# Two-layer decoder step on one core: VectorE instead of GpSimd forms the weight-block sums of the down phases, and the ends of the MLP phases are reordered

## What is computed

```python
x = x + mix                                   # output projection of the mixer
h = rmsnorm(x, p['norm_mlp'][layer])
x = x + jnp.square(jax.nn.relu(h @ p['mlp_up'][layer])) @ p['mlp_down'][layer]   # 1024 -> 4096 -> 1024
# layer 0: h = rmsnorm(x, p['norm_mix'][1]) and the projections of layer 1's mixer follow
# layer 1: y = rmsnorm(x, p['norm_final']) follows, and is the output
```

## Time and profile before

| | us |
|---|---|
| median of 3 runs | 3350.61 (3347.99 to 3360.74) |
| the profiled execution, time | 3352.3 |
| its span | 3350.2 |
| PE busy | 3192.0 (95%) |
| DVE busy | 2122.2 (63%) |
| ACT busy | 1165.8 (35%) |
| POOL busy | 1279.1 (38%) |
| mean granted clock of PE | 0.977 |

### The profile page before, as it was taken

One profiled execution on the slowest core, in us unless ns is written; L12 is line 12 of the kernel. 1 busy time (PEld: TensorE's weight loads), 2 busy tenths in 40 slices (PEclk: granted clock), 3 DMA queues, 4 the chain that ended last, 5 costly groups with the idle time before them and its releaser, 6 DMA issues. The chain is left out here.

```text
span 3350.2 us, 74980 instructions
## 1 busy us (share of the span) xinstructions
PE 3192.0 (95%) x31716; PEld 3017.6 (90%) x31716; DVE 2122.2 (63%) x2892; ACT 1165.8 (35%) x2373; POOL 1279.1 (38%) x760
## 2 busy tenths in 40 slices
PE   8999889999999988999999989999998999999997
PEld 7999768888887888999999989999998899999997
DVE  5112874664665748666777784566546966667776
ACT  3344122332332334444333342221222444443333
POOL 3322120110113025444677733222211544457783
PEclk9999899999999999999999989999999999999998
DMA  5113630100011102444544411111112144454442
GB/s 170 59 58 109 190 118 9 33 30 16 30 36 48 67 30 74 142 143 143 201 147 146 131 46 57 66 63 59 59 60 112 58 137 145 143 199 144 144 146 82
DMA packets 151199, 322.70 MB, mean 96 GB/s; under 512 B 16904, under 2 KB 50356, under 8 KB 150744
## 3 DMA queue, kind: packets, MB, share of 16 engines
q1 hardware_dynamic: 106480, 242.53, 22.3%
q10 hardware_dynamic: 44392, 75.42, 6.6%
HBM read 227.12 MB, written 93.12 MB: 96 GB/s over the span
## 5 line engine op out<-in xcount | busy, mean ns | idle before, releaser
L247 PE MATMUL psum<-act_hi,w_hi 128*128 128x352 f32 x2088 | 704.7, 337 | 21.2 <-DVE act_lo L4169 5.7
L232 POOL TENSOR_TENSOR w_hi<-w_raw,derived 128x1024 fp32r<-128x1024 f32 x87 | 169.4, 1947 | 1415.6 <-PE psum L247 1339.3
L247 PE MATMUL psum<-act_hi,w_lo 128*128 128x352 f32 x2088 | 677.7, 325 | 0.0
L247 PE MATMUL psum<-act_lo,w_hi 128*128 128x352 f32 x2088 | 676.6, 324 | 0.0
L247 PEld LDWEIGHTS psum<-act_hi,w_hi 128*128 128x128 f32 x2088 | 397.1, 190 | 49.8 <-issue 15.2
L247 PEld LDWEIGHTS psum<-act_lo,w_hi 128*128 128x128 f32 x2088 | 398.7, 191 | 2.5 <-issue 0.2
L247 PEld LDWEIGHTS psum<-act_hi,w_lo 128*128 128x128 f32 x2088 | 397.9, 191 | 0.0
L1072 PE MATMUL psum<-ff_near,ff_w_hi 128*128 128x264 f32 x2048 | 382.7, 287 | 8.9 <-ACT ff_a L1202 5.9
L1072 PEld LDWEIGHTS psum<-ff_near,ff_w_hi 128*128 128x128 f32 x2048 | 320.0, 190 | 15.5 <-issue 15.1
L1072 PE MATMUL psum<-ff_far,ff_w_hi 128*128 128x264 f32 x1536 | 285.9, 287 | 12.3 <-DVE ff_r L1407 6.2
L1072 PE MATMUL psum<-ff_near,ff_w_lo 128*128 128x264 f32 x1024 | 292.7, 286 | 0.0
(11 more groups left out here) (556 smaller groups left out, 7496.5 us busy)
## 6 DMA issues: line engine op xcount, KB each, us to landing
ff_du_raw<-u SPq DMA_DIRECT2D x224, 264.0 KB, 2.8
w_raw<-weights SPq DMA_DIRECT2D x87, 512.0 KB, 3.3
u<-ff_stage SPq DMA_DIRECT2D x128, 264.0 KB, 2.2
ff_raw<-mlp SPq DMA_DIRECT2D x64, 512.0 KB, 3.9
u<-ff_side SPq DMA_DIRECT2D x96, 264.0 KB, 3.7
s_cache<-cache_a ACTq DMA_DIRECT2D x32, 512.0 KB, 6.8
ff_dt<-mlp SPq DMA_DIRECT2D x64, 256.0 KB, 4.4
ff_dt<-mlp SPq DMA_DIRECT2D x32, 512.0 KB, 7.1
```

The lines of the kernel that those rows point to most:

```text
L232: pool.tensor_tensor(hi, raw, self.zeros, ALU.add).then_inc(s.sem, s.step())
L247: last = pe.matmul(out, w[:, k, :], h[:, k, cols], start=(start and k == ks[0] and m == 0), stop=(stop and k == ks[-1] and m == 2))
```

## The change

It has five parts. The tables and orders that only say which row comes when are shown by two lines.

1. **Down phases**: DVE forms all sums of weight blocks (S1 to S4, all groups). They stand behind the adds of a step: S1 and S3 of the first group behind step 0, S1 of the next group behind a group's last step, S3 behind its first, S2 behind the step ahead of product 1, S4 behind the step ahead of product 6. POOL is left with the low parts of weights.
2. **Start of the down phase**: the four `u_lower` of step 1 stand ahead of step 0's adds, and `mixed_last` of the last pair behind step 0's third unit.
3. **Steps 26 and 27**: their high and low parts get buffers of their own ("last") and are written ahead, those of step 27 into DVE's step 25.
4. **First pair of the up phase**: DVE makes the low parts for P5, P3 and P4; the eighth row of squares is no longer added by DVE but by PE (two float32 matmuls for each of the three sums); the quadrants come in the order 22, 12, 11, 21; ACT keeps ff_a of pair 1 ahead of squaring quadrant 21, and ff_b of pair 15 ahead of squaring quadrant 11; POOL waits for the last operand of P4 before it starts on pair 1.
5. **Around the MLPs**: the first four weight tiles of layer 1's mixer are loaded into four buffers during step 25, ACT makes their high parts, POOL the low parts by one subtraction each. The squares of the norm behind either MLP are added in another order, and the final norm takes the middle norm's order.

```diff
     def column_sum(self, engine, steps, g, q):
...
-    def corner_sum(self, pool, g, q):
+    def corner_sum(self, dve, g, q):
...
-        pool.tensor_tensor(a11, self.S1[q][:, :], a11, ALU.subtract).then_inc(steps.sem, steps.step(f"split.{n}.S2_{g}.{q}"))
+        dve.tensor_tensor(a11, self.S1[q][:, :], a11, ALU.subtract).then_inc(steps.sem, steps.step(f"dve.{n}.S2_{g}.{q}"))
...
     def pool(self, pool):
...
         for p in (1, 2, 6, 7):
             self.weight_low(pool, 0, p)
-        for p in (5, 3, 4):
-            self.weight_low(pool, 0, p)
+        pool.wait_ge(*at(f"dve.{n}.lo_T4_1"))
         for w in range(1, self.PAIRS):
...
         for step in range(self.STEPS):
-            g, m = divmod(step, 7)
-            for q in four:
+            for q in range(self.WIDTH):
                 self.w_lower(pool, step, q)
-            if step == 1 or m == 6 and g + 1 < self.GROUPS:
-                for q in four:
-                    self.side_sum(pool, s, 0 if step == 1 else g + 1, q)
-            if g and m == 0:
-                for q in four:
-                    self.column_sum(pool, s, g, q)
-            if self.product_of(step) == 1:
-                for q in four:
-                    self.corner_sum(pool, g, q)
-            if self.product_of(step) == 6:
-                for q in four:
-                    self.row_sum(pool, g, q)
...
     def pe_sum(self, pe):
...
-            pe.matmul(K.psum[:, 6 + c % 2, 0:TC], K.ones[:, :], self.rstd[:, c * TC:(c + 1) * TC], start=True, stop=True)\
-                .then_inc(s.sem, s.step(f"pe.{n}.sum{c}"))
+            cols, out = slice(c * TC, (c + 1) * TC), K.psum[:, 6 + c % 2, 0:TC]
+            pe.matmul(out, K.ones[:, :], self.rstd[:, cols], start=True, stop=False)
+            pe.matmul(out, K.ones[:, :], self.sq_last[:, cols], start=False, stop=True).then_inc(s.sem, s.step(f"pe.{n}.sum{c}"))
...
     def act(self, act):
...
-        for p in (3, 4):
-            self.weight_high(act, 1, p)
+        keep_both(1, 0)
         self.square_out(act, 0, "21")
+        self.weight_high(act, 1, 4)
...
-        self.square_out(act, w, "11")
         self.w_high(act, 0, 1)
         keep_both(w, 1)
+        self.square_out(act, w, "11")
...
+        end, last = self.STEPS - 2, self.STEPS - 1
+        for q in range(self.WIDTH):
+            self.w_high(act, end, q)
         for q in range(2):
-            self.w_high(act, self.STEPS - 1, q)
+            self.w_high(act, last, q)
         for q in range(self.WIDTH):
-            self.u_high(act, self.STEPS - 1, q)
-            if q >= 2:
-                self.w_high(act, self.STEPS - 1, q)
+            self.u_high(act, end, q)
+        for q in range(2, 4):
+            self.w_high(act, last, q)
+        for q in range(self.WIDTH):
+            self.u_high(act, last, q)
+        if self.following is not None:
+            self.following.act_weights(act)
...
     def dve_step(self, dve, k, c):
...
-        add(7)
         self.weight_sum(dve, 0, 4)
...
+        for p in (5, 3):
+            self.weight_low(dve, 0, p)
...
     def dve(self, dve):
...
-        self.mixed_last(dve, w)
+        for q in range(self.WIDTH):
+            self.u_lower(dve, 1, q)
         for step in range(self.STEPS - 2):
             for j, d in enumerate(self.UNITS):
                 self.down_add(dve, step, d)
-                if j < 2:
-                    for q in (2 * j, 2 * j + 1):
+                if step == 0 and j == 2:
+                    self.mixed_last(dve, w)
+                for q in (2 * j % 4, 2 * j % 4 + 1):
+                    if 0 < step and j < 2:
                         self.u_lower(dve, step + 1, q)
-            if step == 0:
-                for q in range(self.WIDTH):
-                    self.column_sum(dve, s, 0, q)
+                    elif step == self.STEPS - 3:
+                        self.u_lower(dve, step + 2, q)
+            g, m = divmod(step, 7)
+            p = self.product_of(step)
+            ahead = self.product_of(step + 1)
+            for q in range(self.WIDTH):
+                if step == 0 or m == 6 and g + 1 < self.GROUPS:
+                    self.side_sum(dve, s, g + 1 if step else 0, q)
+            for q in range(self.WIDTH):
+                if m == 0:
+                    self.column_sum(dve, s, g, q)
+            for q in range(self.WIDTH):
+                if ahead == 1:
+                    self.corner_sum(dve, g, q)
+                elif ahead == 6:
+                    self.row_sum(dve, g, q)
...
+    def act_weights(self, act):
+
+        s = self.K.plan.steps["act"]
+        act.wait_ge(self.K.sem("w_loaded"), 16 * (self.w0 + 4))
+        for n in range(4):
+            for label in self.first_free[n]:
+                act.wait_ge(*self.K.plan.at(label))
+            act.activation(flat(self.K.slots[self.slot(0, n)][0]), self.first_raw[n][:, :], ACT.Copy)\
+                .then_inc(s.sem, s.step(f"act.C.weight{n}"))
```

213 lines of the change are left out of this document (123 added, 90 removed).

## The result

The changed kernel takes 3317.41 us (median; 3312.52 to 3323.26), the kernel before 3350.61: a ratio of 0.9893, 95% interval 0.9873 to 0.9913. The forecast was 3306, with a range of 3294 to 3333. The profiled executions took 3352.3 and 3316.99 us, spans of 3350.2 and 3315.2: 35 us, of 45.1 forecast. The forecast was right in sign, and the time lies in the range, 1.4 us outside the band of 3298 to 3316 that the prediction had given a chance of 0.45. Ten microseconds are missing.

The account below looks back on a forecast made before the run. PE, busy 95% of the span, was taken as the bound; gains 20.4 + 2.4 + 10.2 - 1.2 + 5.9 + 7.4 = 45.1 us off the profiled 3352.3 gave 3307.2, by the median 3306; range 3294 to 3333.

Parts of the forecast that it names:

- First pairs: First two pairs of the up phase: removed waits make pair 1 end 10.2 us earlier, 20.4 in both MLPs.
- step-by-step count: Pair 0 of the up phase, followed through VectorE's order: P4 ends at 1309.9 instead of 1315.0.
- Last pair: Last pair of the up phase: ff_b kept ahead of squaring quadrant 11 removes waits in two places; gain 2.4 us.
- Start of the down phase and steady part: Down phases: reordered first steps gain 10.2 us in both MLPs; moved sums cost 1.2 us in the steady part.
- lower case: Down phase, step 2: GpSimd's low parts held up by loads, most sums run free, wait 0.4 us rather than 2.6.
- Rival (a): Steady down phase: no slack at changes of group, 1.5 us waits plus half clock, 25 us in all, 3329; chance 0.17.
- Rival (e): Steady down phase: VectorE gains nothing from GpSimd's lighter load, 11 us over in each MLP, 3328; chance 0.06.
- End of ff0: Last units and norm's sum behind ff0: 34.9 us instead of 40.8, a gain of 5.9 us.
- The two spells at half clock: End of ff0: PE runs at half clock twice as before, 5.2 us in all.
- End of ff1: ff1's 16 last units in 25.8 us instead of 30.7, the rest 14.0 instead of 16.5; gain 7.4 us.

Follow-up runs that it names:

- e1: Changed kernel, but ACT keeps ff_b of pair 1 ahead of squaring quadrant 11, not behind it; 3316.69 us.
- e9: Changed kernel, mixer weights 2 and 3 in exchanged buffers; pair 1's ff_b, ff_c and quadrant 22 ahead of what waits for pair 2's weights; 3306.11 us.
- e10: e9, but in pair 0 VectorE forms quadrant 11 behind the four weight sums for pair 1; 3312.2 us.
- e12: Changed kernel, mixer weights 2 and 3 in exchanged buffers; pair 1's ff_b, ff_c kept before squaring quadrant 11, POOL's product 4 low part before 5, 3; 3310.99 us.
- e5: Kernel before with part 2 alone (step 1's low parts first, mixed_last behind step 0's third unit); 3345.95 us.
- e4: Changed kernel with part 1 alone undone, the sums of weight blocks back on POOL; 3317.3 us.
- e8: Changed kernel, but in steps 3 to 24 two of DVE's four low parts are made twice, 44 more per MLP; 3341.7 us.
- e7: Changed kernel, but POOL starts the mixer's first low parts only behind step 27's low parts; 3313.96 us.
- e11: Changed kernel, but POOL makes each of the mixer's first four low parts in two instructions of 128 x 512; 3315.83 us.
- e2: Changed kernel, but weights 2 and 3 of layer 1's mixer exchange their buffers; 3313.17 us.
- e6: Changed kernel, but POOL, not DVE, makes pair 0's low parts for products 5, 3 and 4; 3311.29 us.

## Why the prediction was right or wrong

**First pairs: half right, 11 us short.** For pair 0 the step-by-step count held: P4 waits 0.33 us and ends 25.4 us behind the first matmul, where the text had it at 1309.9, 25.3 behind. PE needs 3.3 us for the twelve sum instructions, 3.6 in the count. The step that failed is the sentence "Pair 1 then finds its low parts, its bank and ff_a ready, and ends at 1330.4". It checked what pair 1 begins with, not what its later products wait for: in the kernel before, pair 0's mixed squares, the low parts and the load for pair 2 had run while PE stood. Pair 1 ended 51.0 us behind the first matmul, not 46. P5, the product of 24 matmuls ahead of which PE waits for ff_b, ended 8.0 us behind the product before it instead of 2.9: 3.36 us of waiting, and most of the rest at half clock. e1, e9, e10 and e12 show that it is no single wait: each one removed brings up the next, through DVE, ACT, POOL, SP's queue and a load.

**Last pair: 2.4 us forecast for both MLPs, about 1 measured.** ff_b is there, and PE then waits 0.69 and 0.66 us for ff_c, where it waited 1.15 and 1.42. The term took the removed wait as the gain without the next product.

**Start of the down phase and steady part: 11.6 instead of 9.0, the mechanism half right.** No wait of over 0.3 us is left in ff0, one of 0.56 in ff1. The text put the gain at the start on the order of part 2. e5 shows that this order alone only moves the waits to step 2; it takes part 1 (2 us per MLP, e4) and the 1.1 us by which DVE comes earlier into the phase. The text had 9.5 us for the eight sums behind step 0, the first four beside POOL at 1.72 each; they took 5.5, POOL standing idle for 3.95 us of them. That was its lower case. In the steady part I forecast 1.2 us of waiting and there was none; DVE was busy for 0.85 of it, not 0.9. Rival (a) named the right place and mechanism, as e8 shows, but at a load that only e8 reached. Rival (e) fell: moving 52 sums (48 in the text) added 31 us to DVE, 0.6 each, since its low parts came down from 1.38 and 1.35 us to 0.94 and 1.11 with less of POOL beside them. The Trainium skill ("Perfetto Trace Analysis", section "Optimizing Scalar/DVE Operations") warns that moving work between the two might not help. For the whole time that fits: with the sums back on GpSimd it was 3317.3 us against 3317.4 (e4).

**End of ff0: 9.2 instead of 5.9.** The low parts came 2.84 us late, 2.0 in the text. (Its nine and thirteen adds behind them make 9.6 us, not the 9.8 written.) The sum of squares cost 1.03 and not 3.6: I had set its arrival against PE's time without PE's own waits and its half clock. PE was later by these, and what it had already lost there it could not lose again. The two spells at half clock, 5.2 us in the sum, were one: PE's matmuls stood 0.22 instead of 0.12 us apart from 10.8 to 16.5 us behind step 25, about 2.6 us. Waits of PE in one chain are not to be added up when the later one ends at a time of its own. e7 and e11 confirm this: with the first waits gone or down to 0.47 us, the third grew by more than they had been (to 6.69 and 4.96), since the sum came 20.0 and 19.0 us behind step 25, little earlier than the 20.6 of the change. And behind these longer waits PE took 12.5 and 12.9 us to the end of the stretch instead of 11.0, so that nothing was gained. No run takes part 3 or part 5 out alone: that the 9.2 us come from them is read from the waits, 4.09 before and 2.84 now for the low parts, 7.03 and 1.03 for the sum.

**End of ff1: right, in both terms.** The 16 units took 26.0 us and what stands behind them 13.9, together 39.9; the forecast was 25.8 + 14.0 = 39.8. PE waited 1.02 us for the sum among the units (1.1 in the text), and the 19 y tiles took 9.51 us, forecast 9.5. Here too no run takes a part out alone.

**The mixer: not seen, 3.3 us.** The turned buffers were in the diff, and I had followed them only to their first use. e2 takes the loss back in full.

## What to carry to other kernels

When a change takes PE's waits away in a tight stretch, follow each engine through the next two iterations, not one: what the wait had hidden (here stores, low parts and a load for the pair after next) becomes the next wait, and fixing the named releaser moved it one product on here (3.36 us to 4.29). When buffers or slots are renumbered, look up who takes them over at the far end of the phase and in which order. And price a moved instruction by what the other engine does at that moment: here eight sums cost 5.5 us at a time when GpSimd was mostly idle, and four cost 6.3 beside it.

## What the runs showed of the hardware

- VectorE's wait behind GpSimd follows the length of GpSimd's instruction: an instruction of VectorE with both inputs in SBUF took about 0.7 us alone, 1.6 to 1.8 beside GpSimd's 128 x 512 and 2.2 to 2.6 beside its 128 x 1024 (changed kernel, e7, e11). The Trainium skill ("SBUF — State Buffer", section "SBUF: two separate sides") has this as a lock that the one that starts first holds for its whole instruction, and these runs agree.
- It works the other way too. While VectorE ran scalar_tensor_tensor instructions back to back, one GpSimd instruction of 128 x 512 took 6.38 us (e6) and 7.53; beside a series of tensor_tensor instructions on 128 x 528 it took 1.6 to 1.9 (e4, e5, e9). Whether the kind of instruction or its inputs make the difference was not tried.
- The part ahead of ff0, untouched in all fourteen kernels, took 1275.8 to 1286.9 us in the profiled executions. Its cause was not looked for; it is larger than most of the effects studied here.
